# The expert stage in 24 rounds of 128 rows, four column blocks of TensorE, instead of 32 experts of 96 rows

## The reference, cut to what matters

```
for block of rows, e in expert order:
    xb  = x_pad[toks]                                            # rows x 1024
    out = (silu(xb @ w_gate[e]) * (xb @ w_up[e])) @ w_down[e]    # 1024 -> 256 -> 1024
y[token] += out * weight
```

## Time and profile before

| what | us |
|---|---|
| median of 3 timed runs | 1147.45 (1146.6 to 1147.6) |
| the profiled execution's own time | 1149.03 |
| its span, first to last instruction | 1147.2 |
| TensorE busy in the span | 1058.0 (92%) |
| weights of one expert in MB | 3.15 |

### The profile page before, as it was taken

How to read it: one execution, slowest core, us unless ns; L and a number is a source line. 1 busy time by engine, 2 the same in 40 slices (tenths; PEclk the granted TensorE clock), 3 DMA queues, 4 the chain that set the end, 5 groups by cost and what they waited for, 6 DMA issues and landing times. The chain is left out here.

```text
span 1147.2 us, 16445 instructions
## 1 busy us (share of the span) xinstructions
PE 1058.0 (92%) x6188; PEld 720.4 (63%) x6188; DVE 563.5 (49%) x1247; ACT 423.5 (37%) x1003; POOL 260.2 (23%) x326
## 2 busy tenths in 40 slices
PE   6999989999988999999997888799999999999980
PEld 3643334444555777777785455587878787878760
DVE  3406699999838678888835641214111111111114
ACT  2315534877544555656631343111111111111114
POOL 3740116644400111100006110011212121212110
PEclk9999989999996999999997999799999999999995
DMA  8600000000281111311111671599999999999928
GB/s 269 227 22 1 1 18 1 27 16 0 71 220 49 56 56 33 152 38 56 47 54 70 262 294 72 176 374 323 343 333 347 332 348 333 342 336 341 281 32 322
DMA packets 51342, 191.42 MB, mean 167 GB/s; under 512 B 10926, under 2 KB 13950, under 8 KB 41029
## 3 DMA queue, kind: packets, MB, share of 16 engines
q1 hardware_dynamic: 39583, 142.71, 35.0%
q0 software_dynamic: 11536, 47.71, 14.7%
q10 hardware_dynamic: 158, 0.16, 0.1%
HBM read 162.49 MB, written 28.19 MB: 166 GB/s over the span
## 5 line engine op out<-in xcount | busy, mean ns | idle before, releaser
L1585 PEld LDWEIGHTS ps<-mem 128*128 128x128 f32 x2048 | 236.6, 194 | 16.8 <-issue 16.8
L1661 ACT ACTIVATE mem<-ps 128x512 f32<-128x512 f32 (+9 forms) x368 | 160.6, 472 | 228.7 <-PE ps L1378 50.8
L1585 PE MATMUL ps<-mem 128*128 128x96 f32 x2048 | 236.0, 277 | 0.8 <-DVE mem L2606 0.8
L2165 DVE TENSOR_SCALAR_CACHE_REDUCE mem<-mem 128x768 bf16<-128x768 f32 (+2 forms) x134 | 166.5, 1282 | 0.0
L1591 PE MATMUL ps<-mem 128*96 128x512 f32 x256 | 117.6, 601 | 2.5 <-DVE mem L2598 2.5
L1426 PE MATMUL ps<-mem 128*128 128x256 f32 x512 | 117.0, 381 | 1.2 <-DVE mem L2448 1.0
L2598 DVE TENSOR_TENSOR mem<-mem,ps 128x192 f32<-128x192 f32 x32 | 11.4, 355 | 212.9 <-ACT mem L2041 212.9
L1045 POOL DMA_INDIRECT h_rows<-mem x32 | 46.5, 1454 | 296.0 <-DVE mem L2613 296.0
L2041 ACT ACTIVATE mem<-ps 128x192 f32<-128x192 f32 x32 | 10.6, 332 | 262.6 <-PE ps L1585 262.6
L1426 PEld LDWEIGHTS ps<-mem 128*128 128x128 f32 x512 | 94.9, 190 | 14.5 <-ACT mem L1661 1.1
L1591 PEld LDWEIGHTS ps<-mem 128*96 128x96 f32 x256 | 39.0, 162 | 57.1 <-issue 51.2
(11 more groups left out here) (309 smaller groups left out, 1451.3 us busy)
## 6 DMA issues: line engine op xcount, KB each, us to landing
mem<-in_expert_w_gate SPq DMA_DIRECT2D x32, 1024.0 KB, 5.1
mem<-in_expert_w_up SPq DMA_DIRECT2D x32, 1024.0 KB, 8.8
mem<-in_expert_w_down SPq DMA_DIRECT2D x32, 1024.0 KB, 13.2
mem<-in_x_prompt SPq DMA_DIRECT2D x16, 512.0 KB, 4.2
mem<-in_w_in SPq DMA_DIRECT2D x3, 2048.0 KB, 10.6
h_rows<-mem SPq DMA_DIRECT2D x8, 512.0 KB, 2.6
xn_rows<-mem SPq DMA_DIRECT2D x8, 512.0 KB, 2.9
mem<-h_rows SPq DMA_DIRECT2D x8, 512.0 KB, 5.9
```

The costliest lines, as they stand in the source:

```text
L1585: ins = mm(ps[:, 2 + s, j * CAP:(j + 1) * CAP], wgu[w][:, j // 2, k, (j % 2) * P:(j % 2 + 1) * P], xgT[:, s, k, :], start=(k == 0), stop=( ...
L1661: return fn(out, in_, ACT.Copy, scale=scale)
L2165: v.tensor_scalar(bufs[a % 3][0:R, 0:w], sc, mid[:, a:a + 1], None, ALU.is_ge, ALU.add, accum_out=cnt[:, a:a + 1]).then_inc(step, 1)
```

## The change

The 32 experts become 24 rounds. In each of the 4 groups, six experts own a round each; rows 0 to 95 of a round are the 96 slots of its own expert. The remaining two experts of each group are shared out: 32 of their 96 slots ride as rows 96 to 127 of each of three successive rounds that belong to another group. A round gathers 128 rows in one indirect DMA, and adds 128 rows in one.

The operands of the gate and up product are swapped. The turned rows are now the stationary operand, in four blocks of 32 rows (`lanes`), and 512 columns of weights (256 of gate and 256 of up) move; each block writes its own 32 partitions of PSUM. Blocks 0 to 2 read the own expert's buffer, block 3 the shared one's. The down product has the same four blocks. The hidden rows come out untransposed, so a new step turns them (`hidden_turn`, two transposes, VectorE copies them out). TensorE's order becomes gate and up of t + 1, hidden turn of t, row turn of t + 2, down of t.

Six weight buffers take the place of four: four for own experts in turn, two for shared ones. Three experts' weights are loaded before the stage instead of two. New small VectorE copies (15, behind `targets`) and three small DMAs write per-round lists of rows, targets and weights. The first round's rows come in two gathers, 96 and 32. `destinations` still follows the first four steps. The overflow branch keeps the old shape.

```diff
 PIECES += [[{"S": 4, "V": 4}] * 3 + [{"S": 1}]]
-WSLOTS = 4
-OSLOTS = 6
+PER_GROUP = NE // 4
+ROUNDS = 24
+OWN_SLOTS, SHARED_SLOTS = (0, 5, 2, 3), (1, 4)
+NSLOTS = 6
 OQ = 4
 UNITS = [(3, 0), (3, 1), (2, 0), (2, 1), "S", (1, 0), (1, 1), (0, 0), (0, 1)]
...
+
+def own(t):
+
+    return PER_GROUP * (t // 6) + t % 6
+
+
+def shared(t):
+
+    g = t // 3
+    return PER_GROUP * ((g // 2 + 2) % 4) + 6 + g % 2
 
 
...
-            return q * (WSLOTS // 2) + u // 2
+        def own_slot(t):
+            return OWN_SLOTS[t % 4]
+
+        def shared_slot(t):
+            return SHARED_SLOTS[t // 3 % 2]
+
+        def of_round(t, kind, rows_=slice(0, P)):
+            n = 24 * (t % 3) + 8 * kind + t // 3
+            col = lists[rows_, n:n + 1]
+            return col if kind == 2 else col.bitcast(U32)
+
+        def rows_landed(t):
+            return 16 * (t // 2 + 1) + (16 if t % 2 == 0 else 0)
...
             copied(sp, "2c", "PV", 0)
-            weights(0, 0)
+            weights(own(0), own_slot(0))
             copied(sp, "2c", "PV", NPAIR - 1)
-            weights(1, 1)
+            weights(shared(0), shared_slot(0))
             tail(NT)
+            weights(own(1), own_slot(1))
+            sp.wait_ge(lists_ready, 1)
+            for r in range(3):
+                sp.dma_start(lists[CAP:P, 24 * r:24 * (r + 1)], shared_list[32 * r:32 * (r + 1), :]).then_inc(lists_in, 16)
             sp.wait_ge(phase2, 4)
 
-            for s in range(2):
-                sp.wait_ge(xg_in[s], 16)
-            weights(2, 2)
-            weights(3, 3)
-            with sp.Fori(1, NE // WSLOTS) as q:
-                for u in range(WSLOTS):
-                    sp.wait_ge(dn_filled[1], q * WSLOTS + (u - WSLOTS + 1))
-                    weights(q * WSLOTS + u, u)
+            tiles_out(sp, h_out, TILES)
+            sp.wait_ge(xg_in[0], rows_landed(0))
+            weights(own(2), own_slot(2))
+            weights(own(3), own_slot(3))
+            weights(shared(3), shared_slot(3))
+            for t in range(ROUNDS):
+                if t + 4 < ROUNDS:
+                    sp.wait_ge(dn_filled[1], t + 1)
+                    weights(own(t + 4), own_slot(t + 4))
+                if t % 3 == 2 and t + 4 < ROUNDS:
+                    weights(shared(t + 4), shared_slot(t + 4))
 
             sp.dma_start(gb[:, :], final_norm_g.rearrange("(a n) -> a n", a=1).partition_broadcast(P)).then_inc(gn_in, 16)
 
-            sp.wait_ge(dn_filled[1], NE)
+            sp.wait_ge(dn_filled[1], ROUNDS)
             sp.wait_ge(dest_ready, 1)
...
+            def rows_of(t):
+                if t >= 2:
+                    pool.wait_ge(xT_filled[1], t - 1)
+                pool.indirect_dma_start(xg[:, t % 2, :], None, xn_dram,
+                                        bass.IndirectOffsetOnAxis(ap=of_round(t, 0), axis=0)).then_inc(xg_in[t % 2], 16)
+
+            def add_round(t):
+                pool.indirect_dma_start(h_dram, bass.IndirectOffsetOnAxis(ap=of_round(t, 1), axis=0),
+                                        ob[:, t % 2, :], None, compute_op=ALU.add).then_inc(eo_out[t % 2], 16)
 
...
 
-            rows_of(0)
+            for rows_, e in ((slice(0, CAP), own(0)), (slice(CAP, P), shared(0))):
+                n = rows_.stop - rows_.start
+                pool.indirect_dma_start(xg[rows_, 0, :], None, xn_dram,
+                                        bass.IndirectOffsetOnAxis(ap=slot_tok[0:n, e:e + 1], axis=0)).then_inc(xg_in[0], 16)
+            pool.wait_ge(lists_in, 48)
             rows_of(1)
             tiles_out(pool, h_out, TILES)
             pool.wait_ge(pads_cleared, 16)
             pool.wait_ge(targets_ready, 1)
-            for e in range(NE):
-                if e + 2 < NE:
-                    rows_of(e + 2)
+            rows_of(2)
+            rows_of(3)
...
+            for t in range(ROUNDS):
+                if t + 4 < ROUNDS:
+                    rows_of(t + 4)
                 for c in range(2):
-                    pool.wait_ge(dn_emptied[c], e + 1)
-                if e:
-                    pool.wait_ge(eo_out[(e - 1) % 2], 16 * ((e - 1) // 2 + 1))
-                add_rows(e, ob[0:CAP, e % 2, :], eo_out[e % 2])
+                    pool.wait_ge(dn_emptied[c], t + 1)
+                if t:
+                    pool.wait_ge(eo_out[(t - 1) % 2], 16 * ((t - 1) // 2 + 1))
+                add_round(t)
             for s in range(2):
-                pool.wait_ge(eo_out[s], 16 * (NE // 2))
...
+            def lanes(t):
+                return [(slice(32 * n, 32 * n + 32), own_slot(t) if n < 3 else shared_slot(t)) for n in range(4)]
+
...
+            def gate_up(t):
+                s = t % 2
+                pe.wait_ge(we_in[own_slot(t)], 48 * (t // 4 + 1))
+                pe.wait_ge(we_in[shared_slot(t)], 48 * (t // 6 + 1))
                 for c in range(2):
-                    pe.wait_ge(xT_emptied[c], e + 1)
-                if above(e, 1):
-                    pe.wait_ge(hid_ready, q * WSLOTS + (u - 1))
-                products(s, u).then_inc(gu_filled, 1)
-
-            def down(q, u):
-                e, s = q * WSLOTS + u, u % 2
-                pe.wait_ge(hid_ready, e + 1)
+                    pe.wait_ge(xT_emptied[c], t + 1)
+                if t >= 2:
+                    pe.wait_ge(hid_ready, t - 1)
...
+                for k in range(KC):
+                    for tok, w in lanes(t):
+                        ins = mm(ps[tok, 2 + s, :].rearrange("p (a n) -> p a n", a=2), xgT[:, s, k, tok], wgu[w][:, :, k, :],
+                                 start=(k == 0), stop=(k == KC - 1))
+                ins.then_inc(gu_filled, 1)
+
+            def hidden_turn(t):
+                pe.wait_ge(hid_ready, t + 1)
+                if t:
+                    pe.wait_ge(hT_emptied, t)
+                for k in range(2):
+                    ins = tr(ps[:, 4, k * P:(k + 1) * P], hid[:, t % 2, k * P:(k + 1) * P], ident(P))
+                ins.then_inc(hT_filled, 1)
+
+            def down(t):
+                pe.wait_ge(hT_emptied, t + 1)
                 for c in range(2):
-                    if above(e, 0):
-                        pe.wait_ge(dn_emptied[c], e)
-                    down_half(s, u, c).then_inc(dn_filled[c], 1)
-
-            def experts(q, last=False):
-                for u in range(WSLOTS):
-                    gate_up(q, u)
-                    if u < WSLOTS - 1:
-                        rows_turn(q, u + 1)
-                    elif not last:
-                        rows_turn(q + 1, 0)
-                    down(q, u)
-
-            rows_turn(0, 0)
-            experts(0)
-            with pe.Fori(1, NE // WSLOTS - 1) as q:
-                experts(q)
-            experts(NE // WSLOTS - 1, last=True)
-
-            pe.wait_ge(dn_emptied[0], NE)
-            pe.wait_ge(dn_emptied[1], NE)
+                    if t:
+                        pe.wait_ge(dn_emptied[c], t)
+                    for k in range(2):
+                        for tok, w in lanes(t):
+                            ins = mm(ps[tok, 5 + c, :], hT[:, t % 2, k, tok], wdn[w][:, k, 512 * c:512 * (c + 1)], start=(k == 0), stop=(k == 1))
+                    ins.then_inc(dn_filled[c], 1)
+
+            rows_turn(0)
+            gate_up(0)
+            rows_turn(1)
+            for t in range(ROUNDS):
+                if t + 1 < ROUNDS:
+                    gate_up(t + 1)
+                hidden_turn(t)
+                if t + 2 < ROUNDS:
+                    rows_turn(t + 2)
+                down(t)
+
+            pe.wait_ge(dn_emptied[0], ROUNDS)
+            pe.wait_ge(dn_emptied[1], ROUNDS)
             pe.wait_ge(dest_ready, 1)
...
+            keep_xgT(0)
+            silu(0)
+            keep_xgT(1)
+            for t in range(ROUNDS):
+                if t + 1 < ROUNDS:
+                    silu(t + 1)
+                if t + 2 < ROUNDS:
+                    keep_xgT(t + 2)
+                keep_out(t)
             act.wait_ge(dest_ready, 1)
...
+                    table = by_group(table[0:CAP, 0:NE])
+                    typed = lambda x: x if kind == 2 else x.bitcast(U32)
+                    for r in range(3):
+                        v.tensor_copy(typed(lists[0:CAP, 24 * r + 8 * kind:24 * r + 8 * kind + 8]).rearrange("p (g v) -> p g v", v=2),
+                                      table[:, :, r:6:3])
+                    to = typed(shared_list[0:CAP, 8 * kind:8 * kind + 8]).rearrange("p (g v) -> p g v", v=2)
+                    v.tensor_copy(to[:, 0:2, :], table[:, 2:4, 6:8])
+                    ins = v.tensor_copy(to[:, 2:4, :], table[:, 0:2, 6:8])
+                ins.then_inc(lists_ready, 1)
...
+            def keep_hT(t):
+                dve.wait_ge(hT_filled, t + 1)
+                if t >= 2:
+                    dve.wait_ge(dn_filled[1], t - 1)
+                v.tensor_copy(hT[:, t % 2].rearrange("p k t -> p (k t)"), ps[:, 4, 0:2 * P]).then_inc(hT_emptied, 1)
+
...
+            def expert_round(t):
+                keep_hT(t)
```

(91 more changed lines are left out.)

137 lines of the change are left out of this document (69 added, 68 removed).

## The result

The changed kernel takes 1101.87 us (median of 4, 1101.61 to 1105.05) against 1147.53 (4 runs, 1146.6 to 1148.22) measured beside it: a ratio of 0.961 [0.959, 0.962]. The gain is 45.7 us.

The account below looks back on a forecast made before the run. The DMA engines were taken to bound the expert stage: last weights at 1076, last addition at 1101 against 1121.45, so 1149.03 - 20.5 = 1128.5, less 1.6 to the median, 1127 us; range 1088 to 1160, the mechanism's own 1105 to 1143.

Parts of the forecast that it names:

- The share of 1.02: DMA engines' busy share in the expert stage before, read as a wall; forecast to stay about 1.0 to the last weights.
- TensorE's round: Expert stage: 24 phases 10.3 us, transposes 1.4, four changes 0.4; 12.1 us a round, 24 of them 290 us against 371.
- The steps "nothing" for ScalarE and VectorE and for the lists: Extra copy a round costs nothing; list copies before the stage delay first transposes perhaps 1 us, inside the roundings.
- The DMA term: Expert stage after 738 us: 91.2 MB at 2.75 plus 23.1 MB at 4.08 us a MB, 338 us; last weights at 1076.
- low bound: DMA transfers of the stage: 302 us, 36 less, if a deeper queue lets weights run at 426 GB/s, 2.35 us a MB.
- The busy share over 1 for 255 us: DMA engines in the stage before: cited against the rival that they are only as busy as asked to be.
- The end: From the last weights' landing: addition 22 out at 1088.2, two additions of 6.4 us, last landing 1101 against 1121.45, 20.5 less.
- Two blocks at a time: Rival, gate, up and down products: only two column blocks overlap, a round 22.4 us, about 1307 us in all; chance 0.13.
- strict order: Rival's second form: a block's second MATMUL holds up the next block's first; 1307 us, within the 0.13.
- The clock falls in the stalls: Rival: TensorE at half clock after waits; one spell costs 3.5 us, hidden; lesser forms 1143 to 1165 us; chance 0.15.
- The rival that gave way: The DMA wall gives way: engines only as busy as asked, 1075, or weights at 426 GB/s, 1091; 1085 to 1105, chance 0.09.
- The test that I named: Prediction wrong if fours start in twos, stage DMA share falls below 0.95, or last weights land before 1050 or behind 1090.

## Why the prediction was right and wrong

*Side, mechanism, bound: right.* Faster, with four blocks at once and the DMA engines as the bound; forecast at 0.58 and shown by the fours of loads, by the run with a quarter of the products (9 us) and by the one with a third less weights (38 us). The share of 1.02 came too, but is no proof. The size was wrong: 45.7 us and not 20.5.

*TensorE's round: right.* 11.70 us against 12.1. The transposes take 1.06 and 0.44 us, and going from one form to the other costs next to nothing. The steps "nothing" for ScalarE and VectorE and for the lists held: the first gate and up starts at 737.72. On GpSimd's queue an addition takes 10.4 us and a gather 8.6 to land (12.4 and 13.9 feared).

*The DMA term: this step failed.* I wrote "This wall does not move", and took the prices of before, 2.75 and 4.08 us a MB, 338 us in all. They measured 2.44 and 3.67, and the term 300 to 302 us, at the low bound that I had given it for another reason (stretches with few gathers). Two things were in the old prices. The larger: 32 gathers into partitions 0 to 95, which slow everything beside them. The change removed these with the shape of its rounds, and I counted its gathers by bytes alone. With gathers of 96 rows the capacity is 352 GB/s, with whole ones 377 to 383, so 25 to 31 of the 39 GB/s. The smaller is the rest of 8 to 14 GB/s: with a quarter of the products the same gathers left 352 GB/s, so before the engines were not at their limit. Whether TensorE's loads have a part in this rest is not shown. I took "The busy share over 1 for 255 us" as a proof of the limit; it is none, as 340, 349, 352 and 383 GB/s all come with a share of 1.01 to 1.03. At 352 GB/s the 114.5 MB would have taken 325 us.

*The end: too short by 11 us.* I let gate and up of round 23 start when the last weights land. It starts 10 us behind them (1047.82, after 1038): a shared set is needed by three rounds at once, so TensorE gets its last stall at 1022 and then has three rounds before it, while the DMA engines have only two own sets left. From that start to the last landing it took 26.3 us (forecast 24.9). Landing to landing: 38 us less than forecast from the DMA term, 11 more from this one, 27 in all; the last addition landed at 1074.1 and not at 1101.

*The rivals.* Two blocks at a time, and strict order: against both, four at once, if the program puts the four side by side. The rule that MATMULs start and end strictly in program order stands in the Trainium skill ("TensorE: Matmul & The Clock Gate", The mechanism; the forecast named the section behind it). The run with the loops exchanged goes against it: by the rule a seam would save one phase, and it saves four (22.59 us and not 26.2). The clock falls in the stalls as I said, costs 1.7 to 2.0 us in the two shown (3.5 forecast), and is hidden behind the DMA engines. The rival that gave way, 1085 to 1105, holds the measured time, and I had put 0.09 on it: its second half (faster weights) was right, for a reason that it didn't have; that it holds the time is in part luck. The test that I named, last weights before 1050, caught the error.

*Still open.* Why partitions 0 to 95 are worse than whole gathers: by the map no port gets more rows than with 128. The run with 96 and 32 rows has the same bytes per port as a whole gather and is still slow, so the total per port doesn't settle it; it also has twice as many gathers, and what their number alone costs was not measured. Nor do the runs tell whether it is the port or the DMA engine that serves a row, as only the partitions were moved. What happens between transfers at one port was not seen.

## What to carry to other kernels

A price per MB taken from a trace holds for the shape of the transfers in it; when a change alters which partitions the transfers reach, ask what the old ones cost their neighbours. A DMA share of 1.0 beside a TensorE at 99% tells not which of the two is the wall: compare the GB/s with what the loop asks for, or take work from TensorE and look again. And when one load serves three rounds, count the rounds that are left when its data comes, not only the time of the last byte.

## What the runs showed of the hardware

- With half gathers into partitions 32 to 95 the stage moves 374 GB/s, with the same into 0 to 63 it moves 352 (19 us for 22 gathers). Splitting a gather of 128 rows into 96 and 32 takes the rate from 377 to 341 GB/s.
- Four column blocks of 32, each with float32 products of 512 columns, take no more time than one (7.06 us for 64 MATMULs), if the blocks alternate in the program; block after block the same take 22.59 us, 52 phases for 64: at a seam TensorE starts some four MATMULs of the next block ahead of their turn.
- TensorE's stationary loads are not what held the DMA engines: 407 GB/s in 3 us of unbroken loading, and with whole gathers 383 GB/s beside 834 loads in 270 us, mostly of 128 columns, 380 beside 1144 and 377 beside 2078, mostly of 32.
- The busy share of the DMA engines was 1.01 to 1.03 at every rate from 340 to 383 GB/s.
- Behind a stall of 4.14 us TensorE had 1.2 GHz for some 3.4 of the next 9 us, and it cost 1.7 us.
